# Moving the expert retrievals of a decoder layer: prompt heads 24 steps ahead of their first step in place of 16

## The reference

```python
h2 = rms_norm(x1, norm2_w)
q = (h2 @ w_peer_q).reshape(T, 8, 2, 128)            # 8 heads, 2 halves
s = einsum('thpc,hpkc->thpk', q, sub_keys)            # 128 scores for each half
s1, i1 = top_k(s[:, :, 0], 16); s2, i2 = top_k(s[:, :, 1], 16)
top_s, top_c = top_k(all 256 sums of s1 and s2, 16)
idx = i1[top_c // 16] * 128 + i2[top_c % 16]; g = softmax(top_s)
y = x1 + sum_k g * gelu(h2 . expert_u[idx]) * expert_v[idx]   # 128 experts for each token
```

## Time and profile before

| | |
|---|---|
| median of three runs | 2363.9 us (2360.26 to 2368.31) |
| the profiled execution | 2364.97 us, its span 2363.1 us |
| TensorE busy | 1678.2 us (71%) |
| VectorE busy | 1468.1 us (62%) |
| ScalarE busy | 882.9 us (37%) |
| GpSimd busy | 750.7 us (32%) |
| moved by the DMA engines | 756.64 MB, of which the gathers' queue 570.46 MB |
| first step, last step on VectorE | 595.2 us, 2355.6 us |

### The profile page before, as it was taken

One profiled execution on the slowest core, in us unless ns is written; L12 is line 12 of the kernel. 1 busy time (PEld: TensorE's weight loads), 2 busy tenths in 40 slices (PEclk: granted clock), 3 DMA queues, 4 the chain that ended last, 5 costly groups with the idle time before them and its releaser, 6 DMA issues.

```text
span 2363.1 us, 32781 instructions
## 1 busy us (share of the span) xinstructions
PE 1678.2 (71%) x11544; PEld 770.1 (33%) x11544; DVE 1468.1 (62%) x3591; ACT 882.9 (37%) x2386; POOL 750.7 (32%) x713
## 2 busy tenths in 40 slices
PE   6988899998788887777788889885433343343343
PEld 3455565444334443433444433331000000000000
DVE  1466656212556777777878676535676765676764
ACT  2122123201444544544455662333343333343332
POOL 1244100000222334433343333323444443344342
PEclk9998999999889998898889999996555555555555
DMA  4333435645889888899989999999999999999998
GB/s 170 137 105 105 158 111 216 263 182 191 310 345 383 345 350 326 314 347 358 339 343 359 367 394 397 404 407 371 408 391 405 401 392 376 400 387 399 403 386 362
DMA packets 130191, 756.64 MB, mean 320 GB/s; under 512 B 16836, under 2 KB 42940, under 8 KB 50268
## 3 DMA queue, kind: packets, MB, share of 16 engines
q0 software_dynamic: 78336, 570.46, 61.5%
q1 hardware_dynamic: 51692, 184.09, 21.0%
HBM read 734.70 MB, written 20.64 MB: 320 GB/s over the span
## 4 chain that ended last, share of the span: by engine, by line
DMA 20%; DVE 15%; PE 9%; issue 6%; ACT 3%; POOL 0%; DVEq 0%; POOLq 0%; ACTq 0%
DMA ring<-in_expert_uv,pick 20%; PE z L1141 4%; DVE ring L1843 4%; PE acc L1292 3%; DVE cand L1785 1%; DVE e L1786 1%; DVE cand L1783 1%; DVE ti L1748 1%; DVE ti L1751 1%; DVE sco L1749 1%; ACT wgt L1455 1%; ACT fold L1457 1%; DVE tv L1750 1%; DVE ci L1751 1%; DVE ci L1748 1%
## 5 line engine op out<-in xcount | busy, mean ns | idle before, releaser
L1073 POOL DMA_INDIRECT ring<-in_expert_uv,pick x544 | 628.1, 1155 | 1012.2 <-PE acc L1292 935.1
L1843 DVE CUSTOM_DVE_ANT_0 ring<-ring,rep 128x1024 f32<-128x1024 f32 x544 | 660.3, 1225 | 379.1 <-DMA ring<-in_expert_uv,pick 354.5
L1292 PE MATMUL acc<-ring,fold 128*32 128x256 f32 x4352 | 464.0, 517 | 496.9 <-ACT fold L1457 495.0
L1141 PE MATMUL z<-wts,hT 128*128 128x384 f32 (+1 forms) x1408 | 628.4, 583 | 31.7 <-DVE tmp L1907 25.3
L1453 ACT ACTIVATE gel<-dots 128x1 f32<-128x1 f32 x544 | 109.8, 202 | 790.7 <-DVE dots L1843 783.2
L1292 PEld LDWEIGHTS acc<-ring,fold 128*32 128x32 f32 x4352 | 105.3, 126 | 822.1 <-ACT fold L1457 746.8
L1141 PEld LDWEIGHTS z<-wts,hT 128*128 128x128 f32 x1408 | 263.8, 203 | 288.6 <-issue 229.4
L1141 PE MATMUL z<-wts,yT 128*128 128x512 f32 x384 | 192.2, 636 | 14.3 <-ACT yT L1631 7.0
L1457 ACT ACTIVATE fold<-cst,wgt 128x32 f32<-128x32 f32 x544 | 174.8, 321 | 17.7
L1455 ACT ACTIVATE wgt<-gel,pick 128x1 f32<-128x1 f32 x544 | 160.3, 295 | 17.7
L1740 DVE SCALAR_TENSOR_TENSOR yT<-uT,vec,yT 128x256 f32<-128x256 f32 x240 | 109.2, 504 | 2.0
(11 more groups left out here) (219 smaller groups left out, 1745.2 us busy)
## 6 DMA issues: line engine op xcount, KB each, us to landing
wts<-in_w_qkv SPq DMA_DIRECT2D x24, 1536.0 KB, 8.2
wts<-in_w_glu SPq DMA_DIRECT2D x8, 2048.0 KB, 12.2
wts<-in_w_gate SPq DMA_DIRECT2D x8, 2048.0 KB, 11.6
wts<-in_w_wq SPq DMA_DIRECT2D x8, 2048.0 KB, 11.7
ring<-in_k_cache SPq DMA_DIRECT2D x8, 1536.0 KB, 9.4
ring<-in_v_cache SPq DMA_DIRECT2D x8, 1536.0 KB, 8.1
rep<-x_h SPq DMA_DIRECT2D x68, 128.0 KB, 9.9
ring<-in_expert_uv,pick POOLq DMA_INDIRECT x544, 11.3
```

The lines of the kernel that those rows point to most:

```text
L1073: eng.indirect_dma_start(ring[:, i % RING, :], None, a["expert_uv"], bass.IndirectOffsetOnAxis(picks(i, 0).bitcast(U32), 0)).then_inc(row_ ...
L1141: mm = eng.matmul(bank[:, 0:w], of[:, k, :], rows[:, k, :], start=(k == 0), stop=(k == depth - 1))
L1292: mm = eng.matmul(acc[b][SUB * c:SUB * (c + 1), col:col + 256], fold[:, i % 4, :], ring[:, i % RING, D + 256 * c:D + 256 * (c + 1)], start ...
L1843: eng.tensor_tensor_reduce(u, u, rep[:, j, :], 1.0, 0.0, ALU.mult, ALU.add, dots[:, i % 4:i % 4 + 1]).then_inc(dot_ready, 1)
```

## The change

One expression in `item_list()` gives other steps to the retrievals:

```diff
     for t in STEP_TILES:
         for h in range(PH):
-            at = 8 + 32 * h if t == NT else BASE[t] - 16 + 16 * h
+            at = 16 + 32 * h if t == NT else BASE[t] - 16 if (t, h) == (2, 0) else max(0, BASE[t] - 24 + 16 * h)
             out.append((-1 if (t, h) == (0, 0) else at, t, h))
     return sorted(out)
```

## The result

The kernel with the change took 2387.93 us (median of four runs, 2384.05 to 2389.11); the kernel before, in runs beside it on the same chip, 2362.53 us. The ratio is 1.0088, its 95% interval 1.0061 to 1.0115. That is slower, outside the predicted range of 2344 to 2373 us.

A forecast was written before the change was run, and what follows sets the result against it. The prediction saw DMA engines at least eight tenths busy from slice 11 and nothing but the first gather waiting for picks. Its terms, 0 - 3.6 = -3.6 us, took 2363.9 to 2360.3, rounded 2360; range 2344 to 2373.

The forecast's parts named there:

- No wait for picks: On GpSimd, only the kernel's first gather waits for picks, so the longer lead removes no wait.
- The swap in steps 0 to 272: Eight blocks losing a retrieval and eight gaining one change roles: 17.8 - 17.8 = 0 us.
- The bound of +17.8: Slow end for steps 0 to 272: old blocks give nothing back, new ones pay in full, +17.8 us.
- prediction's signs of being wrong: A gather waiting for picks, one-sided block changes, spread waits under 25 or over 50 us, ticks changing over 7 us.
- The 2.2 us, put down to waits before spreads: Steps 0 to 272: a retrieval costs 2.2 us, from TensorE's 39.2 us of waits for spreads, counted at no change.
- A reading of rows 1: DMA engines busy at least eight tenths from slice 11, nine from 21; flow creeping from about 345 to 400 GB/s.
- The idle-time rival: Eight new blocks' 97.1 us of idle VectorE take about 91 us of retrieval work: 2342.5, half 2351.4; chance 0.30.
- The spread rival: Spreads stop TensorE at blocks 56, 216 and 24: 2378.1, half 2369.2; sign some 50 us of waits; chance 0.18.
- The tail, put at -3.6: From step 288, two retrievals fall into VectorE's gather waits in blocks 280 and 408, saving 1.8 us each.
- The sign in VectorE's gather waits of block 408: If right, VectorE's wait for gathers in block 408 falls from 17.6 us to about 6 to 8.
- The transfers rival: In the tail, DMA transfers set the time anyway, so both savings go: 0, so 2364; chance 0.14.
- Queues of SyncE and GpSimd: Score loads move with retrievals on SyncE, GpSimd's first gather asks for older picks: counted as nothing.

The follow-up runs named there:

- Undo_four: The changed kernel with four retrievals put back from steps 24, 88, 152 and 184 to 32, 96, 160 and 192: 2370.83 us, 1.0025 of the kernel before.
- short_lumps: The changed kernel, each top 16 taking only its first eight at steps 88, 152 and 184: 2374.42 us, 1.0034 of the kernel before.
- tail_only: The kernel before with only the retrievals from step 288 on moved 8 steps earlier: 2362.77 us, 0.9990 of the kernel before.
- spaced_before: The kernel before with a retrieval's four parts two steps apart, spread and placing three steps later: 2334.04 us, 0.9876 of the kernel before.

## Why the prediction was wrong

**No wait for picks: right.** One wait of 25.6 us, as before. A longer lead had nothing to remove.

**The swap in steps 0 to 272, put at 0: wrong, the step that failed.** The prediction let the two sets of blocks change roles because TensorE's work in them is equal, and so priced a retrieval at 2.2 us from sums over eight blocks. The old blocks gave back 19.3 us, near the bound of 17.8, but the new ones took 37.7, 4.7 us for each retrieval in place of 2.2. Equal work on TensorE was the wrong test. What told the places apart is whether VectorE had 11.4 us to spare in that block; the sum of 97.1 us of idle time hid that three of the eight had 7.5, 5.0 and 7.7. Undo_four shows the places, short_lumps that the length of the lump counts there. The bound of +17.8 was too small as well: a new block can cost more than an old one gives back, as in block 88, where the two engines wait for each other and the granted clock falls to 0.50. Of the prediction's signs of being wrong one came: a change of over 7 us in the ticks.

**The 2.2 us, put down to waits before spreads: wrong too.** These waits fell from 39.2 to 30.4 us (lines below) while the ticks took 15.3 us longer.

**A reading of rows 1 was loose.** The DMA engines stand at nine tenths from slice 22 to 39, and the flow of slices 11 to 21 goes up and down between 310 and 383 GB/s. No term of the sum hangs on it.

**The idle-time rival was the right mechanism with the wrong sum.** It priced lumps by VectorE's idle time, 97 us against 91, over all blocks at once. Block by block, its own rule would have told that five places are free and three are not, though not the sizes.

**The spread rival: near in time (2378), wrong in mechanism.** It named blocks 56, 216 and 24, where TensorE has no air. Their pairs changed by -0.3, -3.0 and +1.1 us. Its sign was spread waits of 50 us or more, from 39.2. Measured, 670 to 1580 us:

```profile
PE o L1274 <- DVE cand L1796: 15.4, 6, 4.5
...
PE o L1274 <- DVE ho L1951: 9.0, 2, 7.5
...
PE o L1274 <- DVEq L1882: 6.0, 2, 3.6
```

They sum to 30.4 us. Waits for steps' weights grew instead, from the first to the second of these lines (670 to 1560 us before, 670 to 1580 after):

```profile
PE acc L1292 <- ACT fold L1457: 36.0, 22, 4.4
...
PE acc L1292 <- ACT fold L1457: 53.4, 26, 8.9
```

In blocks 56 and 216 a TensorE without idle time went with a late VectorE at no loss over the pair. But TensorE's idle time is not the test: block 120 had 8.8 us of it (22.49 busy of 31.3) and its pair changed by -0.2, block 184 had 2.8 and its pair lost 9.9.

**The tail, put at -3.6: not borne out.** The sign in VectorE's gather waits of block 408 came nearly as predicted (6 to 8 us, from 17.6):

```profile
DVE ring L1843 <- DMA ring<-in_expert_uv,pick: 5.5, 3, 3.4
```

But blocks 288 and 416 stayed at 23.7 and 24.2 us (23.6 and 24.7) where 21 to 23 was expected, and tail_only is at 0.9990 with an interval of about 4 us either way. The lump took the place of a wait and the block behind did not get shorter.

**The transfers rival** fits the move in the tail, which won nothing, but not the tail as such: spaced_before shows 14.6 us to be had there. The 358 GB/s limit that the Trainium skill gives ("DMA: Bandwidth & Descriptors", "Where 436 GB/s comes from") is passed by spaced_before's 413 GB/s over 250 us on this core, which runs alone, as by the 420 of rows 5.

**Queues of SyncE and GpSimd, put at 0:** nothing in the traces speaks against it.

What stays open: the order of the heads (some 5 us or none), what holds the pair at 184, and how much of TensorE's longer busy time lies on the path.

## What to carry to other kernels

Price a moved piece of work at each place that it moves to, against the idle time of its own engine there; idle time in one block pays for nothing in another. Work that nothing waits for is better cut into small parts far apart than moved earlier: spacing four parts by two steps gained 1.2% here, eight steps of lead lost 0.9%. Where two engines feed each other, look at what the second one does when the first is late: in block 88 a shared PSUM tile made them take turns.

## What the runs showed of the hardware

After a pause TensorE was slower for a while. After it had stood for most of 945 to 957 us its matmuls ran at a granted clock of 0.50 to 0.55, and the eight of line 1141 took 5.13 us. The kernel before, the same matmuls in its timeline and the stretch that they lie in:

```profile
948.98 2.85 PE L1141 MATMUL z<-wts,hT 128*128 128x384 f32 x8
...
951.99 1.90 PE L1173 MATMUL o<-kvr,pt 128*128 128x64 f32 x16
...
948.90:956.00 7.10, 7.04 (x49) 4.37 (x45) 4.79 (x8) 4.87 (x11) 4.22 (x5) 1.00 0.99 406
```

Over the three pairs TensorE's busy time grew by 11.9 us beside 8.6 us of idle time; in the kernels with half gathers by 12.4 beside 8.6, with 707 and 718 matmul records.

A DMA share of 1 did not mean that the flow was at its limit: the same share went with 399, 413 and 420 GB/s.
